# Table lookups with their row slots written out, and a reordered first row

## The chip, the cores and the metric

The kernel runs on one core of a Trainium2 chip, in one launch. The metric is the device time of that launch in microseconds (us); lower is better. The kernel before took 2431.6 us (median of 3 runs, 2429.14 to 2432.04).

The engines go by their short names: PE (matmuls), DVE (vector), ACT (scalar), POOL (GpSimd, which here issues the gathers) and SP (which issues the weight loads).

## The reference

Two transformer parts follow each other over 256 tokens of width 1024, all in f32: an FFN, latent and block attention and an FFN, then two layers of a mixer (a state-space mixer, then retention), a product-key lookup and a gated embedding. Only the two lookups matter here:

```python
def peer_ffn(h, w_q, sub_keys, u, v):            # T=256 tokens, 8 heads, K=16, NK=128
    q = (xt @ w_q).reshape(T, PEER_HEADS, 2, PEER_HALF)
    sc = jnp.einsum('thcd,hckd->thck', q, sub_keys)
    s1, i1 = lax.top_k(sc[:, :, 0], K)
    s2, i2 = lax.top_k(sc[:, :, 1], K)
    cand = (s1[..., :, None] + s2[..., None, :]).reshape(T, PEER_HEADS, K * K)
    cand_idx = (i1[..., :, None] * NK + i2[..., None, :]).reshape(T, PEER_HEADS, K * K)
    top_s, top_pos = lax.top_k(cand, K)
    idx = jnp.take_along_axis(cand_idx, top_pos, axis=-1)
    gate = jax.nn.softmax(top_s, axis=-1)
    ...
        hid = jax.nn.gelu(jnp.einsum('tkd,td->tk', u[ib], xb), approximate=False)
        return jnp.einsum('tk,tkd->td', (gb * hid), v[ib])
```

Each token and head picks 16 of 16384 rows of `u` and `v`, takes the dot product of the `u` row with the token, and adds up the `v` rows.

## The kernel before, in words

A stage `peer(layer)` does one lookup. The 256 tokens are 2 tiles of 128 partitions; a **row** is one tile and one head, so there are 16 rows, and a row has 16 **slots**, one for each chosen table row: 256 slots in a layer. Buffers for 8 gathered slots stand in SBUF (`SLOTS`), the matrices of the last four slots too (`DIAGS`).

A slot passes through all engines in this order. POOL waits until the buffer is free (`slot_free`) and issues an indirect DMA (L640), 128 descriptors of 8 KB, a `u` row and a `v` row each. DVE waits for it to land (`row_landed`) and takes the dot product (L1837). ACT applies gelu to the 128 sums (L1092). DVE writes a diagonal matrix of gelu times weight (`spread`, L1786). PE multiplies it with the `v` halves into two accumulating banks (L1907) and frees the buffer.

Between these, DVE chooses the experts of the **next** row (`pick`, a generator of 15 steps, one or two of which run in each slot), and ACT takes its softmax (`softmax_exp`, L1042) after slot 7; DVE makes the weights (`weigh`) in slot 10. Beside the slots (`beside`) PE multiplies the queries and scores of heads 2 to 7, for which SP loads a weight unit of 1 MB each, ACT writes its high part (L694) and DVE its low part (`split`, L1186). `HEAD_AT` gives the slot at which each head's product begins: 1, 13, 25, 40, 56, 72.

Row 0 has its own start. DVE copies its scores from a bank (L1676) and finds the first 8 experts (`first_pick`), so that POOL can issue 8 gathers, and the other 8 after them. `row_gain` (L1258) multiplies the token rows by the norm's gain, which the dot products need.

How the slots are written: `peer_rows` (L666) writes pairs of rows 0 to 4 out one after the other (`PAIRS_APART = 5`), and pairs 5 to 7 as one hardware loop of three turns (`Fori`, L670) on PE, DVE and ACT. In the loop the semaphore values to wait for are computed in registers. POOL writes its first pair out and loops seven times over the others (L646). Each engine runs its own program in its own order; nothing but semaphores ties them.

Of the kernel before, what the change touches and what calls it, by code (L numbers as in the profile page):

```python
# [90 lines left out]
SLOTS = 8  # L91
# [3 lines left out]
EARLY_HEADS = 2  # L95
# [7 lines left out]
PAIRS_APART = 5  # L103
# [106 lines left out]
def build(nc, x, pos_row, pos_col, consts_d, ret_consts_d, vecs_d, gains_d, gain_cols_d, wide_d, units_d, conv_d, pt_d, uv0, uv1, out):  # L210
    with ExitStack() as ctx:
# [409 lines left out]
        def _(pool):  # L621
            def gathers(layer):
# [3 lines left out]
                def two_rows(pair, i):  # L626
                    for par in range(2):
                        if pair == 0 and par == 0:
                            pool.wait_ge(expert_early, layer + 1)
                        else:  # L630
                            pool.wait_ge(expert_ready, i * 2 + (layer * (ROWS + 1) + 2 * pair + par + 1))
                        for k in range(TOPK):
# [4 lines left out]
                            pool.wait_ge(slot_free, i * (2 * TOPK) + (done + SLOTS * layer + (2 * pair + par) * TOPK + k + 1))  # L637
# [46 lines left out]
        def _(act):  # L684
# [337 lines left out]
            def peer(layer):  # L1022
# [65 lines left out]
                def two_rows(row, i, slot):  # L1088
                    for par in range(2):
                        for k in range(TOPK):  # L1090
                            act.wait_ge(dot_done, i * (2 * TOPK) + ((layer * ROWS + row + par) * TOPK + k + 1))
                            nc.scalar.activation(act_h[par][:, k:k + 1], hid[par][:, k:k + 1], ACT.Gelu).then_inc(gelu_done, 1)  # L1092
                            if slot is not None:
                                beside(slot + par * TOPK + k)
                            if k == 7:
                                softmax_exp(i * 2 + (row + par + 1))

                peer_rows(act, two_rows)
# [71 lines left out]
        def _(dve):  # L1170
# [460 lines left out]
            def peer(layer):  # L1631
# [79 lines left out]
                def pick(row, par):  # L1711
# [9 lines left out]
                    step(V.tensor_copy(st[:, 0], score[:, bass.ds(row, 1), :].rearrange("p a (c k) -> p (a c) k", c=2)))  # L1721
# [100 lines left out]
                def two_rows(first, i, slots):  # L1822
                    tile = first // PEER_HEADS
                    for par in range(2):
                        row = first + par

                        ahead = pick(i * 2 + (row + 1), 1 - par)
                        n = None
                        if tile == 0:

                            dve.wait_ge(score_act, i * 2 + (9 * layer + row + 2))
                        for k in range(TOPK):
                            slot = k % SLOTS
                            dve.wait_ge(row_landed[slot], i * 64 + 16 * (layer * ROWS * 2 + 2 * row + k // SLOTS + 1))
                            if n is not None:
                                picked(i * 2 + (row + 1), n)
                            V.scalar_tensor_tensor(rows_uv[:, slot, 0:D], rows_uv[:, slot, 0:D], 1.0, xn[:, tile, :], ALU.mult, ALU.mult,  # L1837
                                                   accum_out=hid[par][:, k:k + 1]).then_inc(dot_done, 1)
                            n = next(ahead, None)
                            if k >= 1:  # L1840
                                if n is not None:
                                    picked(i * 2 + (row + 1), n)
                                spread(i * (2 * TOPK) + (row * TOPK + k - 1), par, k - 1)
                                n = next(ahead, None)
# [747 lines left out]
```

## Time and profile before

| | us |
|---|---|
| median of 3 runs | 2431.6 (2429.14 to 2432.04) |
| the profiled execution, its own time | 2434.31 |
| span of that execution, first to last instruction | 2432.5 |
| PE busy | 2112.4 |
| DVE busy | 1729.6 |
| DVE idle before L1837 for a gather | 207.5 in 226 waits |
| ACT busy | 787.0 |
| bytes moved by DMA | 726.75 MB |
| of these by the gathers' queue | 539.00 MB |

The profile is one execution. Times in a row count from the start of the span. A row of the time order has start, length, engine, line, operation, output <- input, and in square brackets how long the engine stood idle before it and what ended that. A row of a stretch has its bounds and length, the busy time of PE, of PE's weight loads (PEld), DVE, ACT and POOL, each with the number of instructions, then the granted clock of PE as a share of full speed, the busy share of the 16 DMA engines and GB/s. A DMA queue's row has packets, MB and its share of the 16 engines' time. In rows, "issue" is idle time that no semaphore or transfer explains. The first lookup stage runs from about 775 to 1466 us, the second from about 1723 to 2392 us.

### The profile page before, as it was taken

The numbers are of one execution on the slowest core, as the hardware profiler recorded it, in microseconds if no ns is written. First come the engines' busy times: TensorE is split into PE (matmuls) and PEld (weight loads), VectorE is DVE, ScalarE is ACT, GpSimd is POOL, SyncE is SP. The second block draws the span as 40 slices with busy tenths as digits, with TensorE's granted clock in tenths as the row PEclk, the third lists the DMA queues.
The fourth block names the chain that finished last, engine by engine and source line by source line (L and its number), as shares of the span: only waits on it lengthen the run. The fifth ranks groups of instructions, "written<-read, shape, count | busy, mean of one in ns | idle before, by whom it ended". The sixth has DMA issues, their size and how long they took to land.

```text
span 2432.5 us, 27876 instructions
## 1 busy us (share of the span) xinstructions
PE 2112.4 (87%) x9134; PEld 1378.4 (57%) x9134; DVE 1729.6 (71%) x3722; ACT 787.0 (32%) x1463; POOL 592.2 (24%) x520
## 2 busy tenths in 40 slices
PE   7999899999999888887886688999888897777877
PEld 7998789989877444432332236977544442222324
DVE  5555665558766878878886686646778888877786
ACT  4334653346564221212111116334412211111114
POOL 0000000000101444444443340000343444443440
PEclk9999999999999999999998899999999999999999
DMA  6554325544325999999998995534799999999995
GB/s 247 189 186 170 129 98 181 190 173 165 139 87 209 420 420 417 403 420 408 408 412 342 379 400 228 188 141 156 300 420 420 401 409 420 405 420 415 408 421 210
DMA packets 101205, 726.75 MB, mean 299 GB/s; under 512 B 11616, under 2 KB 11744, under 8 KB 13280
## 3 DMA queue, kind: packets, MB, share of 16 engines
q0 software_dynamic: 74016, 539.00, 54.2%
q1 hardware_dynamic: 25200, 181.41, 20.5%
q10 hardware_dynamic: 1872, 4.88, 0.6%
q8 instruction: 60, 0.98, 0.2%
q14 instruction: 57, 0.47, 0.1%
HBM read 724.21 MB, written 1.05 MB: 298 GB/s over the span
## 4 chain that ended last, share of the span: by engine, by line
PE 23%; DMA 20%; DVE 14%; issue 14%; ACT 2%; POOL 1%; DVEq 0%; POOLq 0%; ACTq 0%; SPq 0%
PE bank L1907 22%; DMA arena<-in_uv,expert 19%; DVE arena L1786 3%; DVE arena L1837 2%; POOL arena L640 1%; DVE arena L1759 1%; DVE arena L1763 1%; DVE sel_i L1765 1%; DVE top_i L1737 1%; DVE arena L1729 1%; DVE top_i L1727 1%; DVE top_v L1732 0%; DVE lw_rounded L1186 0%; DVE arena L1742 0%; DVE top_v L1724 0%
## 5 line engine op out<-in xcount | busy, mean ns | idle before, releaser
L1907 PE MATMUL bank<-arena 128*128 128x512 f32 (+4 forms) x2416 | 1075.1, 579 | 261.4 <-DVE arena L1786 254.9
L1907 PEld LDWEIGHTS bank<-arena 128*128 128x128 f32 (+2 forms) x2416 | 421.1, 194 | 825.7 <-DVE arena L1786 519.9
L640 POOL DMA_INDIRECT arena<-in_uv,expert x512 | 581.5, 1136 | 1175.2 <-PE bank L1907 667.6
L1837 DVE SCALAR_TENSOR_TENSOR arena<-arena,xn 128x1024 f32<-128x1024 f32 x512 | 626.6, 1224 | 243.3 <-DMA arena<-in_uv,expert 207.5
L1186 DVE TENSOR_TENSOR lw_rounded<-lw,w_hi 128x2048 fp32r<-128x2048 f32 x169 | 389.4, 2306 | 222.0 <-ACT w_hi L694 218.8
L1092 ACT ACTIVATE act_h<-hid 128x1 f32<-128x1 f32 x512 | 103.6, 203 | 1055.5 <-DVE arena L1837 1055.1
L1907 PE MATMUL bank<-xT_hi,w_hi 128*128 128x256 f32 x1320 | 414.3, 314 | 4.2 <-DVE xT_lo L1227 4.2
L694 ACT ACTIVATE w_hi<-lw 128x2048 fp32r<-128x2048 f32 x169 | 323.4, 1915 | 260.7 <-PE bank L1907 235.5
L1907 PE MATMUL bank<-xT_hi,lw_rounded 128*128 128x256 f32 x1320 | 374.5, 284 | 0.0
L1907 PE MATMUL bank<-xT_lo,w_hi 128*128 128x256 f32 x1320 | 374.5, 284 | 0.0
L1907 PEld LDWEIGHTS bank<-xT_hi,w_hi 128*128 128x128 f32 x1320 | 253.6, 192 | 28.9 <-issue 25.9
L1907 PEld LDWEIGHTS bank<-xT_lo,w_hi 128*128 128x128 f32 x1320 | 253.4, 192 | 23.8 <-issue 23.0
L1907 PEld LDWEIGHTS bank<-xT_hi,lw_rounded 128*128 128x128 f32 x1320 | 253.3, 192 | 0.1
L1907 PE MATMUL bank<-w_hi,arena_rounded 128*128 128x512 f32 (+1 forms) x680 | 228.8, 407 | 2.4 <-DVE arena_rounded L1203 2.4
L1786 DVE TENSOR_SCALAR arena<-consts,act_h,weight 128x128 f32<-128x128 f32 x512 | 180.9, 353 | 26.8 <-ACT act_h L1092 6.4
L656 POOL TENSOR_TENSOR arena<-arena,vecs 128x2048 f32<-128x2048 f32 x2 | 9.3, 4644 | 602.2 <-ACT arena L694 602.2
L1907 PE MATMUL bank<-w_hi,xT_hi 128*128 128x512 f32 (+2 forms) x368 | 144.6, 393 | 11.7 <-DVE xT_lo L1249 6.5
L1907 PEld LDWEIGHTS bank<-w_hi,arena_rounded 128*128 128x128 f32 x680 | 129.4, 191 | 34.8 <-issue 3.8
L1907 PE MATMUL bank<-w_hi,xT_lo 128*128 128x512 f32 (+2 forms) x368 | 139.0, 378 | 0.0
L1907 PE MATMUL bank<-lw_rounded,xT_hi 128*128 128x512 f32 (+2 forms) x368 | 138.9, 377 | 0.0
L1907 PE MATMUL bank<-lw_rounded,arena_rounded 128*128 128x512 f32 (+1 forms) x340 | 134.9, 397 | 0.0
L1907 PEld LDWEIGHTS bank<-w_hi,xT_hi 128*128 128x128 f32 x368 | 70.1, 190 | 27.9 <-DVE xT_lo L1249 7.6
(249 smaller groups left out, 1486.4 us busy)
## 6 DMA issues: line engine op xcount, KB each, us to landing
lw<-in_units SPq DMA_DIRECT2D x169, 1024.0 KB, 4.8
arena<-in_uv,expert POOLq DMA_INDIRECT x512, 12.2
wide<-in_wide POOLq DMA_DIRECT2D x2, 1024.0 KB, 10.5
gain<-in_gains ACTq DMA_DIRECT2D x4, 512.0 KB, 6.7
wide<-in_units SPq DMA_DIRECT2D x2, 1024.0 KB, 7.6
h<-in_x SPq DMA_DIRECT2D x2, 512.0 KB, 6.1
arena<-in_ret_consts ACTq DMA_DIRECT2D x1, 1024.0 KB, 4.7
out<-xn SPq DMA_DIRECT2D x2, 512.0 KB, 2.6
```

Source lines behind the costliest of these rows:

```text
L640: nc.gpsimd.indirect_dma_start(out=rows_uv[:, slot, :], out_offset=None, in_=table, in_offset=bass.IndirectOffsetOnAxis(ap=expert[par][:, ...
L694: return nc.scalar.activation(o, i, ACT.Copy)
L1092: nc.scalar.activation(act_h[par][:, k:k + 1], hid[par][:, k:k + 1], ACT.Gelu).then_inc(gelu_done, 1)
L1186: V.tensor_tensor(w_lo[:, u % RING, :], lw[:, u % RING, :], w_hi[:, no % HIGHS, :].bitcast(F32), ALU.subtract).then_inc(lo_ready, 1)
L1727: step(V.max_index(top_i[:, c, 0:8], top_v[:, c, 0:8], st[:, 0, c]))
L1729: step(V.match_replace(st[:, 1, c], top_v[:, c, 0:8], st[:, 0, c], LOWEST))
L1737: step(V.max_index(top_i[:, c, 8:], top_v[:, c, 8:], st[:, 1, c]))
L1759: step(V.tensor_tensor(hot[:, c], sel_f[:, c].unsqueeze(2).to_broadcast([P, TOPK, TOPK]), marks.unsqueeze(1).to_broadcast([P, TOPK, TOPK]) ...
L1763: step(V.tensor_tensor(hot[:, c], hot[:, c], top_f[:, c].unsqueeze(1).to_broadcast([P, TOPK, TOPK]), ALU.mult))
L1786: V.tensor_scalar(diag[:, k % DIAGS, :], ident, act_h[par][:, k:k + 1], weight[par][:, k:k + 1], ALU.mult, ALU.mult).then_inc(diag_ready, 1)
L1837: V.scalar_tensor_tensor(rows_uv[:, slot, 0:D], rows_uv[:, slot, 0:D], 1.0, xn[:, tile, :], ALU.mult, ALU.mult, accum_out=hid[par][:, k:k ...
L1907: return nc.tensor.matmul(o, lhsT, rhs, start=start, stop=stop, **more)
```

## The change

All 16 rows of both layers are written out on PE, DVE, ACT and POOL; the loops L646 and L670 and the register arithmetic of their waits are gone. Besides, at the start of each lookup stage: `row_gain` of the first tile stands ahead of `first_pick`; the low part of the weight unit of head 2 (the third head) moves on DVE from ahead of the first slot into slot 1; the choice for row 1 begins in slot 2 of row 0, and with it the wait for the scores of head 1 (`score_act`); on ACT the first softmax comes ahead of the high part of that unit, and the copy of head 1's scores goes behind the first gelu.

```diff
-PAIRS_APART = 5
+
+SECOND_FROM = 2
...
-                two_rows(0, 0)
-                with pool.Fori(0, ROWS // 2 - 1) as i:
-                    two_rows(1, i)
+                for pair in range(ROWS // 2):
+                    two_rows(pair)
...
-        def peer_rows(eng, rows):
-
-            for pair in range(PAIRS_APART):
-                rows(2 * pair, 0, 2 * TOPK * pair)
-            with eng.Fori(0, ROWS // 2 - PAIRS_APART) as i:
-                rows(2 * PAIRS_APART, i, None)
+        def peer_rows(rows):
+
+            for pair in range(ROWS // 2):
+                rows(2 * pair, 2 * TOPK * pair)
...
+                softmax_exp(0)
                 split(first + 4)
-                softmax_exp(0)
-                for i in range(1, EARLY_HEADS):
-                    queries(i)
-                    scores(i)
+                queries(1)
...
                 def beside(slot):
 
+                    if slot == 0:
+                        scores(1)
...
+                row_gain((N_PEER0, N_PEER1)[layer], 0)
                 first_pick()
-                row_gain((N_PEER0, N_PEER1)[layer], 0)
                 weigh(0, 0)
-                split(first_unit + 4)
...
-                        if slot == at - 3:
+                        if slot == max(at - 3, 1):
                             split(first_unit + 1 + head + 1)
...
-                        ahead = pick(i * 2 + (row + 1), 1 - par)
-                        n = None
-                        if tile == 0:
-
-                            dve.wait_ge(score_act, i * 2 + (9 * layer + row + 2))
+                        ahead = pick(row + 1, 1 - par)
+                        n, start = None, SECOND_FROM if row == 0 else 0
                         for k in range(TOPK):
                             slot = k % SLOTS
-                            dve.wait_ge(row_landed[slot], i * 64 + 16 * (layer * ROWS * 2 + 2 * row + k // SLOTS + 1))
+                            if tile == 0 and k == start:
+                                dve.wait_ge(score_act, 9 * layer + row + 2)
+                            dve.wait_ge(row_landed[slot], 16 * (layer * ROWS * 2 + 2 * row + k // SLOTS + 1))
...
-                            n = next(ahead, None)
+                            n = next(ahead, None) if k >= start else None
```

In the order of instructions below, a row is line, operation, output <- input, size, and the semaphores that it waits for. Line numbers of the changed kernel are lower by 3 or 5 around here (L1837 is L1832, L1786 is L1783).

**DVE at the start of the first layer's choice.** L1792 prepares constants, L1676 reads the first scores. Before:

```order
L1634 MEMSET arena 128x256
L1791 COPY consts<-consts 128x8 [waits dve_order]
L1792 TENSOR_SCALAR consts<-consts 128x8
L1676 COPY arena<-bank6 128x256 [waits first_scores,dve_order]
L1679 MAX top_v<-arena 128x8 [waits first_read]
```

Now:

```order
L1788 COPY consts<-consts 128x8 [waits dve_order]
L1789 TENSOR_SCALAR consts<-consts 128x8
L1255 TENSOR_TENSOR xn<-xn,gain 128x1024 [waits gain_loaded1,dve_order]
L1673 COPY arena<-bank6 128x256 [waits first_scores,dve_order]
L1676 MAX top_v<-arena 128x8 [waits first_read]
```

The gain (L1258, now L1255) stands ahead of the copy of the scores.

**DVE from the end of the first choice (L1673, now L1670) into the first slots.** Before:

```order
L1673 SCALAR_TENSOR_TENSOR expert0<-sel_i 128x8 [waits dve_order]
L1258 TENSOR_TENSOR xn<-xn,gain 128x1024 [waits gain_loaded1]
L1774 RECIPROCAL exp_inv<-exp_sum 128x1 [waits exp_ready,dve_order]
L1776 TENSOR_SCALAR weight0<-exps,exp_inv 128x16 [waits top_order]
L1186 TENSOR_TENSOR lw_rounded<-lw,w_hi 128x2048 [waits hi_ready]
L1837 SCALAR_TENSOR_TENSOR arena,hid0<-arena,xn 128x1024 [waits row_landed0,score_act]
L1721 COPY arena<-arena 128x256
L1837 SCALAR_TENSOR_TENSOR arena,hid0<-arena,xn 128x1024 [waits top_order,row_landed1]
L1724 MAX top_v<-arena 128x8 x2
L1786 TENSOR_SCALAR arena<-consts,act_h0,weight0 128x128 [waits slot_free,gelu_done,top_order]
L1727 MAX_INDEX top_i<-top_v,arena 128x8 x2
L1729 MATCH_REPLACE arena<-top_v,arena 128x128 x2
```

Now:

```order
L1670 SCALAR_TENSOR_TENSOR expert0<-sel_i 128x8 [waits dve_order]
L1771 RECIPROCAL exp_inv<-exp_sum 128x1 [waits exp_ready]
L1773 TENSOR_SCALAR weight0<-exps,exp_inv 128x16 [waits top_order]
L1832 SCALAR_TENSOR_TENSOR arena,hid0<-arena,xn 128x1024 [waits row_landed0]
L1832 SCALAR_TENSOR_TENSOR arena,hid0<-arena,xn 128x1024 [waits row_landed1]
L1783 TENSOR_SCALAR arena<-consts,act_h0,weight0 128x128 [waits slot_free,gelu_done]
L1183 TENSOR_TENSOR lw_rounded<-lw,w_hi 128x2048 [waits hi_ready]
L1832 SCALAR_TENSOR_TENSOR arena,hid0<-arena,xn 128x1024 [waits row_landed2,score_act]
L1718 COPY arena<-arena 128x256
L1783 TENSOR_SCALAR arena<-consts,act_h0,weight0 128x128 [waits slot_free,gelu_done,top_order]
L1721 MAX top_v<-arena 128x8 x2
L1832 SCALAR_TENSOR_TENSOR arena,hid0<-arena,xn 128x1024 [waits top_order,row_landed3]
```

Gain and low part (L1186, now L1183) are gone from ahead of the first dot product; the low part stands behind the first `spread`, and the choice for row 1 begins with the copy behind the third dot product.

**DVE at the place where the first layer's loop begins.** Before, with the loop's head (L670) and register instructions (`REGISTER_ALU`, `ISA`):

```order
L1837 SCALAR_TENSOR_TENSOR arena,hid1<-arena,xn 128x1024 [waits row_landed7]
L1786 TENSOR_SCALAR arena<-consts,act_h1,weight1 128x128 [waits slot_free,gelu_done] x2
L670 UNCONDITIONAL_BRANCH
L670 ISA
L1837 SCALAR_TENSOR_TENSOR arena,hid0<-arena,xn 128x1024 [waits row_landed0]
L1721 ISA
L1721 COPY arena<-arena 128x256
L1780 ISA [waits row_landed1]
L1837 SCALAR_TENSOR_TENSOR arena,hid0<-arena,xn 128x1024 [waits top_order]
L1724 MAX top_v<-arena 128x8 x2
L1780 REGISTER_ALU
L1784 ISA [waits top_order]
```

Now:

```order
L1832 SCALAR_TENSOR_TENSOR arena,hid1<-arena,xn 128x1024 [waits row_landed7]
L1783 TENSOR_SCALAR arena<-consts,act_h1,weight1 128x128 [waits slot_free,gelu_done] x2
L1832 SCALAR_TENSOR_TENSOR arena,hid0<-arena,xn 128x1024 [waits row_landed0]
L1718 COPY arena<-arena 128x256
L1832 SCALAR_TENSOR_TENSOR arena,hid0<-arena,xn 128x1024 [waits top_order,row_landed1]
L1721 MAX top_v<-arena 128x8 x2
L1783 TENSOR_SCALAR arena<-consts,act_h0,weight0 128x128 [waits slot_free,gelu_done,top_order]
L1724 MAX_INDEX top_i<-top_v,arena 128x8 x2
```

The branch and the register instructions are gone; the waits stand on the working instructions.

## Rows read from the trace of the kernel before

**Rows 1.** The page: span, engine share, DMA share in 40 slices.

```profile
span 2432.5 us, 27876 instructions
PE 2112.4 (87%) x9134; PEld 1378.4 (57%) x9134; DVE 1729.6 (71%) x3722; ACT 787.0 (32%) x1463; POOL 592.2 (24%) x520
...
DMA  6554325544325999999998995534799999999995
```

**Rows 2.** Both lookup stages: length, PE, PEld, DVE, ACT, POOL busy, clock, DMA, GB/s.

```profile
777.00:1466.00 689.00, 556.78 (x1472) 245.59 (x1472) 542.84 (x1447) 129.37 (x362) 293.16 (x256) 0.95 0.99 402
1725.00:2392.00 667.00, 541.00 (x1465) 240.13 (x1465) 540.97 (x1442) 128.99 (x361) 286.48 (x255) 0.98 1.01 413
```

**Rows 3.** Waits of DVE: who, for whom, total us, times, longest.

```profile
DVE arena L1837 <- issue: 22.0, 2, 11.0
```

**Rows 4.** DVE in time order, first layer: around both jumps back, and the loop's end.

```profile
1287.45 0.35 DVE L1786 TENSOR_SCALAR arena<-consts,act_h,weight 128x128 f32<-128x128 f32 x1 [0.45 <-ACT act_h L1092]
1298.79 1.22 DVE L1837 SCALAR_TENSOR_TENSOR arena<-arena,xn 128x1024 f32<-128x1024 f32 x1 [11.00 <-issue]
...
1376.10 0.35 DVE L1786 TENSOR_SCALAR arena<-consts,act_h,weight 128x128 f32<-128x128 f32 x1 [0.45 <-ACT act_h L1092]
1387.46 1.22 DVE L1837 SCALAR_TENSOR_TENSOR arena<-arena,xn 128x1024 f32<-128x1024 f32 x1 [11.01 <-issue]
...
1465.02 0.35 DVE L1786 TENSOR_SCALAR arena<-consts,act_h,weight 128x128 f32<-128x128 f32 x1 [0.45 <-ACT act_h L1092]
```

**Rows 5.** The same in the second layer.

```profile
2233.75 0.79 DVE L1786 TENSOR_SCALAR arena<-consts,act_h,weight 128x128 f32<-128x128 f32 x2
2235.10 1.23 DVE L1837 SCALAR_TENSOR_TENSOR arena<-arena,xn 128x1024 f32<-128x1024 f32 x1 [0.56 <-DMA arena<-in_uv,expert]
...
2313.88 0.79 DVE L1786 TENSOR_SCALAR arena<-consts,act_h,weight 128x128 f32<-128x128 f32 x2
```

**Rows 6.** DMA from 1287 to 1312 us: share in 40 slices; instruction queue.

```profile
DMA  9999999999999999999997210000000000077799
...
q14 instruction: 4, 0.03, 0.3%
```

**Rows 7.** DMA queues from 820 to 1206 us, rows written out.

```profile
q14 instruction: 11, 0.09, 0.1%
```

**Rows 8.** Stretches in the loops, and one of written-out rows (last).

```profile
1206.30:1286.30 80.00, 65.62 (x127) 23.53 (x125) 63.46 (x171) 12.23 (x39) 35.44 (x32) 0.91 1.01 414
...
2153.00:2233.00 80.00, 60.33 (x127) 21.88 (x126) 62.91 (x171) 12.22 (x39) 33.07 (x32) 1.00 1.01 416
2233.00:2313.00 80.00, 62.37 (x129) 22.91 (x128) 63.96 (x175) 12.43 (x40) 35.42 (x32) 0.98 1.01 411
...
2115.00:2153.00 38.00, 28.77 (x61) 9.96 (x60) 32.17 (x92) 7.54 (x25) 15.55 (x16) 1.00 1.01 421
```

**Rows 9.** DVE before the first slots of both layers, in time order.

```profile
768.98 0.17 DVE L1792 TENSOR_SCALAR consts<-consts 128x8 f32<-128x8 f32 x1
770.45 0.42 DVE L1676 COPY arena<-bank 128x256 f32<-128x256 f32 x1 [1.30 <-PE bank L1907]
...
785.72 1.22 DVE L1258 TENSOR_TENSOR xn<-xn,gain 128x1024 f32<-128x1024 f32 x1
...
787.31 2.29 DVE L1186 TENSOR_TENSOR lw_rounded<-lw,w_hi 128x2048 fp32r<-128x2048 f32 x1
790.10 1.22 DVE L1837 SCALAR_TENSOR_TENSOR arena<-arena,xn 128x1024 f32<-128x1024 f32 x1 [0.50 <-ACT arena L694]
...
1718.32 0.42 DVE L1676 COPY arena<-bank 128x256 f32<-128x256 f32 x1 [1.58 <-PE bank L1907]
```

**Rows 10.** DMA queues from 777 to 806 us.

```profile
q0 software_dynamic: 1151, 8.43, 72.9%
q1 hardware_dynamic: 432, 3.15, 26.2%
```

**Rows 11.** DVE at the ninth slot of the first row.

```profile
812.93 1.23 DVE L1837 SCALAR_TENSOR_TENSOR arena<-arena,xn 128x1024 f32<-128x1024 f32 x1 [0.71 <-DMA arena<-in_uv,expert]
```

More of the change, by code:

```diff
@@ L630, in two_rows @@
                         else:
-                            pool.wait_ge(expert_ready, i * 2 + (layer * (ROWS + 1) + 2 * pair + par + 1))
+                            pool.wait_ge(expert_ready, layer * (ROWS + 1) + 2 * pair + par + 1)
                         for k in range(TOPK):
@@ L1086, in beside, with two_rows @@
                         high_tile((N_PLE0, N_PLE1)[layer], 0, (slot - HIGH_AT,))
-                def two_rows(row, i, slot):
+                def two_rows(row, slot):
                     for par in range(2):
                         for k in range(TOPK):
-                            act.wait_ge(dot_done, i * (2 * TOPK) + ((layer * ROWS + row + par) * TOPK + k + 1))
+                            act.wait_ge(dot_done, (layer * ROWS + row + par) * TOPK + k + 1)
                             nc.scalar.activation(act_h[par][:, k:k + 1], hid[par][:, k:k + 1], ACT.Gelu).then_inc(gelu_done, 1)
-                            if slot is not None:
-                                beside(slot + par * TOPK + k)
+                            beside(slot + par * TOPK + k)
                             if k == 7:
-                                softmax_exp(i * 2 + (row + par + 1))
-                peer_rows(act, two_rows)
+                                softmax_exp(row + par + 1)
+                peer_rows(two_rows)
             def ple(layer):
@@ L1719, in pick @@
                     flat = [cand[:, i].rearrange("p a b -> p (a b)") for i in range(2)]
-                    step(V.tensor_copy(st[:, 0], score[:, bass.ds(row, 1), :].rearrange("p a (c k) -> p (a c) k", c=2)))
+                    step(V.tensor_copy(st[:, 0], score[:, row, :].rearrange("p (c k) -> p c k", c=2)))
                     yield 1
@@ L1820, in add_tile, with two_rows @@
                     add_to_h([(2 * tile + c, tile, c * BANK) for c in range(2)])
-                def two_rows(first, i, slots):
+                def two_rows(first, slots):
                     tile = first // PEER_HEADS
@@ L1840, in two_rows @@
                             if k >= 1:
                                 if n is not None:
-                                    picked(i * 2 + (row + 1), n)
-                                spread(i * (2 * TOPK) + (row * TOPK + k - 1), par, k - 1)
-                                n = next(ahead, None)
+                                    picked(row + 1, n)
+                                spread(row * TOPK + k - 1, par, k - 1)
+                                n = next(ahead, None) if k >= start else None
@@ L1845, in two_rows @@
                             if k == 10:
-                                weigh(i * 2 + (row + 1), 1 - par)
-                            if slots is not None:
-                                beside(slots + par * TOPK + k)
-                        spread(i * (2 * TOPK) + (row * TOPK + TOPK - 1), par, TOPK - 1)
-                peer_rows(dve, two_rows)
+                                weigh(row + 1, 1 - par)
+                            beside(slots + par * TOPK + k)
+                        spread(row * TOPK + TOPK - 1, par, TOPK - 1)
@@ L2465, in beside, with two_rows @@
                         turn_tile((N_PLE0, N_PLE1)[layer], 0)
-                def two_rows(row, i, slots):
+                def two_rows(row, slots):
                     tile = row // PEER_HEADS
@@ L2470, in two_rows @@
                         for k in range(TOPK):
-                            pe.wait_ge(diag_ready, i * (2 * TOPK) + ((layer * ROWS + row + par) * TOPK + k + 1))
+                            pe.wait_ge(diag_ready, (layer * ROWS + row + par) * TOPK + k + 1)
                             for c in range(2):
@@ L2475, in two_rows @@
                             ins.then_inc(slot_free, 1)
-                            if slots is not None:
-                                beside(slots + par * TOPK + k)
-                peer_rows(pe, two_rows)
+                            beside(slots + par * TOPK + k)
+                peer_rows(two_rows)
             def ple(n):
```

7 lines of the change are left out of this document (4 added, 3 removed).

## The prediction

> **What bounds the kernel now.** I read the page first, for where the DMA engines are full. The span is 2432.5 us, PE is busy for 87% of it, and that invites a wrong reading: in slices 13 to 23 and 29 to 38 (counted from 0), the two lookups, the DMA digit is 9 or 8, and PE and DVE only keep up with the gathers [rows 1]. The second view was the busy time by stretch. The first lookup stage, 777 to 1466 us, moves 402 GB/s, the second, 1725 to 2392 us, does the same work in 667 us at 413 GB/s [rows 2]. Undisturbed written-out rows reach 421 GB/s [rows 8]. So a lookup stage costs its bytes over some 420 GB/s, plus the time in which the DMA engines run dry. An edit here is worth what it takes from the dry time, and nothing else: a shorter DVE or ACT path that ends before the next gather lands only makes DVE wait longer for it.
>
> The third view was DVE's waits, to find who lets the DMA engines run dry. One line stands out: two waits for nothing that the profile shows, 11.0 us each [rows 3]. In order of time they lie in the first layer only, between the last diagonal of a row and the first dot product of the next, where DVE's loop L670 jumps back [rows 4]. In that time no diagonal is made, PE frees no buffer and POOL has nothing to issue; the transfers under way go on until 1300 us and then stop: the DMA digits are 2, 1 and then ten zeros of 0.6 us each, and in the same stretch four packets go over the instruction queue [rows 6]. That is an instruction fetch: the code to which DVE jumps has to be brought in again. In the second layer the same jump leaves DVE waiting 0.56 us, for a gather [rows 5]. In written-out rows, 820 to 1206 us, 11 packets of instructions come and none makes DVE wait [rows 7, 3].
>
> **The price of the loops, step by step.** An iteration of the loop is two rows. From the end of the last diagonal before a jump to the same point one iteration on, the first layer takes 1376.45 - 1287.80 = 88.65 us and 1465.37 - 1376.45 = 88.92 us [rows 4], start plus length. The second layer takes 2314.67 - 2234.54 = 80.13 us for the same work without the pause [rows 5]. The pauses of 11 us each cost 8.5 and 8.8 us at the end; the rest is covered by transfers already issued. Sum 17.3 us. The whole stages say the same: 689 us at 402 GB/s are 277.0 MB, at the other stage's 413 GB/s 670.7 us, 18.3 us less, in which other differences between the layers are included [rows 2]. I take 17.3. This is the whole of the main term, and it is in one layer only. What is late next there is what is late in the second layer: the gather's landing, 0.56 us.
>
> The second term is the register arithmetic of the loop's waits. In the second layer's loop the rate is 416 and 411 GB/s over 80 us each, in the first layer's first iteration 414, against 421 in written-out rows [rows 8]. Against 420 that is (4/420 + 9/420 + 6/420) x 80 = 3.6 us for three of the six iterations, so 7 us at most if the register instructions were the cause of all of it, and nothing if it is the dense half of each row (choice steps beside dot products), which the written-out rows have as well. Written-out rows differ in this too, so I take 1.7 us, nearer to nothing. That the code is longer afterwards (six more rows on three engines, fourteen on POOL) costs fetches of the kind in rows 7: 8 KB each in a stream of 420 GB/s, 0.02 us.
>
> By the Trainium skill, "Runtime: NRT & Kernel Launch", section "Instruction fetch mechanics", straight code is streamed ahead and its block crossings are mostly hidden, while a taken branch to a block outside the current window must fetch first. The trace agrees for written-out rows and for the first layer's jumps, and does not for the second layer's, which cost nothing; had both layers' jumps stalled as the rule may be read, the gain would be 35 us. The section also gives 16 KiB blocks; here four packets of 8 KB come at one jump [rows 6].
>
> **The reordered start.** Four edits, in each layer, one answer. The gain's product takes 1.22 us [rows 9]. Ahead of the first choice it falls into a time in which DVE waits for the first scores: 1.30 us before 770.45 and 1.58 us before 1718.32 [rows 9]. It fits in both, in the first layer by 0.08 us, so the first gather is issued where it was, or up to 0.1 us later. Behind the choice DVE then drops 1.22 us for the gain, 2.29 us for the low part of head 2 and the 0.50 us wait for the scores of head 1 [rows 9]: the first dot product moves from 790.10 to about 786.4 us. Slot 1 takes the low part, so the third dot product comes at least 3.7 - 2.3 = 1.4 us earlier than before, somewhat more since the choice's first steps now stand behind it, and with it the freeing of the first buffers. The exponentials needed for the first weight must be ready then; ACT now makes them before the high part instead of after it, and even in the old order they did not hold DVE, whose only idle time there is the 0.50 us. The moved wait for head 1's scores stands ahead of the third dot product, and all later slots queue behind it on DVE; the scores were there at 790.10, some 2 us before it is reached.
>
> What does the end see of that? The ninth gather is issued some 2 us earlier, but the DMA engines are not dry there: from 777 to 806 us they move 8.43 MB of gathers and 3.15 MB of weight units [rows 10], which is 11.6 MB or 27.6 of 29 us at 420 GB/s. By the ninth slot DVE waits for the landing, 0.71 us [rows 11], and the head start has become a longer wait. The choice for row 1 now ends after the tenth dot product instead of the eighth. POOL needs it with the buffer of the ninth slot, whose diagonal DVE writes just behind that point, so it is not late. I take 0 for all four. Bounds: +0.2 us for both layers if the gain delays the first choice; -7.4 us if the whole 3.7 us moved through to the end twice.
>
> **The sum.** 17.3 + 1.7 + 0 = 19.0 us. The profiled execution took 2434.31 us, 1.8 us more than its span, which the change leaves alone: 2415.3. The median of the runs shown is 2.7 us lower, so for timed runs 2431.6 - 19.0 = 2412.6 us.
>
> **Rivals.**
> The head start arrives (A). Mechanism: with buffers freed earlier, the queue of gathers is deeper through the dense rows 1 to 5, where the DMA engines also run dry now and then; the second stage has 667 us where 275.5 MB at 420 would take 656, and the first keeps about as much once its pauses are gone [rows 2]. For it: these 11 us a layer are there to be had. Against: DVE waits for gathers in the second half of each row, which forgets the head start. Time: 2412.6 - 7 = 2405.6.
>
> The pauses go but part comes back (B). The first layer's rows 12 to 15 would have dry spells of their own, as the second layer has with no pause (411 GB/s over 80 us), hidden now because all buffers are full after a pause. For it: the second layer shows them. Against: the comparison of iterations already includes them. If 5 of the 19 us return: 2417.6.
>
> The change does nothing to the pauses (C). If the fetch were not caused by the jump but by something at this place in the stream, the written-out code would meet it too: 2431.6 less 1.7, about 2430. Against: both pauses stand at a jump, none in 20 written-out rows.
>
> Slower (D). Written-out code misses its fetch where the loop of the second layer ran from what was there. New are 6 rows on DVE, PE and ACT in each layer, about one fetch per row on DVE by the 11 packets in nine rows [rows 7]. Twelve fetches that each held DVE 11 us as a jump does, at 8.7 us each at the end, are 104 us for 17.3 saved. It decides from the third such miss on (26 > 19); at four, 2431.6 + 34.8 - 19 = 2447.4. For it: the queue is full of gathers when the fetch is asked for. Against: 20 written-out rows of the same code under the same load show none, which leaves little room.
>
> **How the numbers follow.** Forecast with all its terms 0.76, A 0.09, B 0.09, C 0.03, D 0.03. No change within 0.2% (4.9 us, about what a measurement of this kernel can tell from none) is C. Faster takes forecast, A and B: 0.94; same 0.03; slower 0.03. Range: low end all of A, 2405; high end B and a spread of 1.5 us between runs, 2419.
>
> **What would show it.** In the profile after: no wait of DVE for "issue" of 11 us; the first lookup stage about 671 us long at 412 GB/s or more; no zeros in the DMA digits between the stage's ends; the second stage 664 to 667 us. The first gather within 0.1 us of where it was relative to the first scores, the first dot product within 1 us of the choice's last instruction (now 4.4 us, 785.72 to 790.10), and a DVE wait for a landing by the ninth slot longer than 0.71 us. I am wrong if the first stage stays above 680 us, if the second gets shorter than 660 or longer than 670 us, or if DVE waits for "issue" in written-out rows.

## The result, and the profile after

The changed kernel takes 2419.4 us (median of 5 runs, 2418.2 to 2420.9), the kernel before 2431.6 (2429.1 to 2434.6, 5 runs beside them); the ratio is 0.995, 95% interval 0.9935 to 0.9965. It is faster by 12.2 us, where 19.0 were forecast (2412.6, range 2405 to 2419). The direction and the main term were right; a cost that the forecast put at almost nothing took back about a third of it and moved the time just outside the range.

The page of the profile after, which answers to [rows 1]: span, engines, DMA share in 40 slices, and the instruction queues.

```profile
span 2417.6 us, 26693 instructions
PE 2100.5 (87%) x9134; PEld 1369.8 (57%) x9134; DVE 1730.7 (72%) x3722; ACT 786.6 (33%) x1463; POOL 584.6 (24%) x520
...
DMA  6554325544325999999999994533899999999994
...
q8 instruction: 64, 1.05, 0.2%
q14 instruction: 58, 0.48, 0.1%
```

Both lookup stages by stretch, which answers to [rows 2] (columns as there):

```profile
774.00:1448.00 674.00, 543.31 (x1473) 239.80 (x1474) 543.21 (x1450) 129.52 (x364) 285.58 (x257) 0.99 1.00 412
1707.00:2379.00 672.00, 546.70 (x1470) 240.62 (x1470) 543.01 (x1449) 129.45 (x365) 288.07 (x256) 0.98 1.00 411
```

From the first packet of a stage's gathers to its last dot product, the first stage went from 685.8 to 670.1 us and the second from 667.5 to 669.3: at 412 and 411 GB/s they are now alike, and the second has become slower. DVE's waits, largest first, no longer have the line of [rows 3]:

```profile
DVE arena L1832 <- DMA arena<-in_uv,expert: 219.9, 233, 3.2
DVE lw_rounded L1183 <- ACT w_hi L692: 217.6, 100, 6.1
DVE arena L1287 <- ACT arena L775: 40.5, 21, 2.0
```

At the place of the first jump [rows 4] DVE now goes from diagonal to dot product with a wait of 0.64 us, for a gather:

```profile
1282.76 0.70 DVE L1783 TENSOR_SCALAR arena<-consts,act_h,weight 128x128 f32<-128x128 f32 x2
1284.10 1.23 DVE L1832 SCALAR_TENSOR_TENSOR arena<-arena,xn 128x1024 f32<-128x1024 f32 x1 [0.64 <-DMA arena<-in_uv,expert]
```

So the pauses went. What is missing shows when row is set beside row, by the start of each row's first dot product. Rows 13 to 15 of the second layer, in the loop before, took 39.9 us each, 16 gathers at 2.49 us; written out they take 40.9. The 2.49 us are what the packets give: 128 descriptors of 8 KB over 16 DMA engines are 8 packets each, at 0.31 us per packet in the trace (that each engine gets 8 is an estimate).

### The profile page after: what moved, and what is told of

Same layout as the page of the kernel before. It is cut to its first block, busy times and chain, and to the rows that moved or that the text cites. A ratio compares the mean times of both kernels' runs of the same rounds, so it can differ in the third digit from the quotient of the medians.

```text
span 2417.6 us, 26693 instructions
## 1 busy us (share of the span) xinstructions
PE 2100.5 (87%) x9134; PEld 1369.8 (57%) x9134; DVE 1730.7 (72%) x3722; ACT 786.6 (33%) x1463; POOL 584.6 (24%) x520
## 4 chain that ended last, share of the span: by engine, by line
PE 23%; DMA 22%; DVE 14%; issue 12%; ACT 2%; POOL 1%; DVEq 0%; POOLq 0%; ACTq 0%; SPq 0%
PE bank L1901 22%; DMA arena<-in_uv,expert 22%; DVE arena L1783 3%; DVE arena L1832 2%; POOL arena L641 1%; DVE top_i L1734 1%; DVE arena L1756 1%; DVE arena L1726 1%; DVE top_i L1724 1%; DVE arena L1760 1%; DVE sel_i L1762 1%; DVE top_v L1729 0%; DVE top_v L1721 0%; DVE lw_rounded L1183 0%; DVE sel_s L1737 0%
## 5 line engine op out<-in xcount | busy, mean ns | idle before, releaser
L1901 PE MATMUL bank<-arena 128*128 128x512 f32 (+4 forms) x2416 | 1062.9, 572 | 257.0 <-DVE arena L1783 250.6
L1901 PEld LDWEIGHTS bank<-arena 128*128 128x128 f32 (+2 forms) x2416 | 413.1, 192 | 817.7 <-DVE arena L1783 522.8
L641 POOL DMA_INDIRECT arena<-in_uv,expert x512 | 573.8, 1121 | 1168.4 <-PE bank L1901 641.7
L1832 DVE SCALAR_TENSOR_TENSOR arena<-arena,xn 128x1024 f32<-128x1024 f32 x512 | 626.9, 1225 | 238.7 <-DMA arena<-in_uv,expert 219.9
L1183 DVE TENSOR_TENSOR lw_rounded<-lw,w_hi 128x2048 fp32r<-128x2048 f32 x169 | 389.4, 2306 | 220.7 <-ACT w_hi L692 217.6
L1783 DVE TENSOR_SCALAR arena<-consts,act_h,weight 128x128 f32<-128x128 f32 x512 | 181.6, 355 | 18.3 <-ACT act_h L1090 9.8
```

What stands on the lines that cost most here:

```text
L641: nc.gpsimd.indirect_dma_start(out=rows_uv[:, slot, :], out_offset=None, in_=table, in_offset=bass.IndirectOffsetOnAxis(ap=expert[par][:, ...
L1183: V.tensor_tensor(w_lo[:, u % RING, :], lw[:, u % RING, :], w_hi[:, no % HIGHS, :].bitcast(F32), ALU.subtract).then_inc(lo_ready, 1)
L1783: V.tensor_scalar(diag[:, k % DIAGS, :], ident, act_h[par][:, k:k + 1], weight[par][:, k:k + 1], ALU.mult, ALU.mult).then_inc(diag_ready, 1)
L1901: return nc.tensor.matmul(o, lhsT, rhs, start=start, stop=stop, **more)
```

## The experiments

All times are medians of 4 to 11 runs, but for two single runs near the end, beside runs of the kernel before on the same chip, whose medians there were 2430.3 to 2432.1 us. "Piece" below is 128 instructions of DVE's code, the 8 KB that one packet of the instruction queue brings.

**The loop's place alone.**

```diff
-            with eng.Fori(0, ROWS // 2 - PAIRS_APART) as i:
+            heads = {eng.engine: 0} if eng.engine == mybir.EngineType.DVE else None
+            with nc.Fori(0, ROWS // 2 - PAIRS_APART, engines=..., head_slot=heads) as i:
```

> The kernel before with one thing changed: the first instruction of DVE's loop in each lookup stage is placed at slot 0 of a block of 256 instructions; nothing is written out and the start is the old one. In the kernel before the loop of layer 0 begins with the last instruction before a boundary of 128 (DVE executes one instruction after the jump and then stands still), so that its 260 instructions touch four pieces of 128, and the loop of layer 1 (267 instructions) touches three. Theory (place of the loop, and written-out code is not free): both 11-us pauses go without any code written out, and rows 10 to 15 keep the 39.9 us per row of layer 1's loop, so 2431.6 - 17.3 = 2414.3 us, range 2412.5 to 2416, some 5 us under the written-out kernel although nothing of its other gains is in. Rival 1 (the jump itself stalls in layer 0 wherever it lies): 2431.6, pauses still there. Rival 2 (pauses go, but they were worth only the 12.2 us that writing out brought): 2419 to 2420.

Measured: 2419.5 us. The 11-us pauses are gone with nothing written out, so the jump itself does not stall. But placing the loop this way makes DVE jump into it, which costs a new wait in each layer. DVE's time order, the first dot product of the loop in both layers:

```profile
1209.42 1.22 DVE L1838 SCALAR_TENSOR_TENSOR arena<-arena,xn 128x1024 f32<-128x1024 f32 x1 [5.30 <-issue]
2141.45 1.22 DVE L1838 SCALAR_TENSOR_TENSOR arena<-arena,xn 128x1024 f32<-128x1024 f32 x1 [5.29 <-issue]
```

The time is what rival 2 gave, but its reason is not: rows 13 to 15 are at 39.9 us here, and the same placing without the jump (the padded loop, below) is 5.5 us faster. That the time equals the changed kernel's is a coincidence of two costs.

**The pauses carried to the other layer.** As above, but `head_slot` 13 and layer 0 alone.

> The kernel before, with DVE's loop of layer 0 alone placed, at slot 13 of a block of 256 instructions. Layer 0's 260 instructions then touch three pieces of 128; layer 1's loop, which stands 109 slots further on modulo 128, comes to slot 122 and its 267 instructions touch four. Theory (the number of pieces of 128 that the body touches decides): the two 11-us pauses vanish from layer 0 and appear in layer 1: stage 0 shrinks from 689 to 671 us, stage 1 grows from 667 to some 684, total 2431.6 - 17.3 + 17.3 = 2431.6, range 2429 to 2434. Rival 1 (something of layer 0 causes the pauses): 2431.6 with the pauses still in layer 0. Rival 2 (any placed loop is free, the neighbour does not matter): 2414.3 with no pause at all.

Measured: 2431.0 us, ratio 1.000 (0.9991 to 1.0009), the pauses in layer 1. DVE there, around both jumps back:

```profile
2213.75 0.79 DVE L1787 TENSOR_SCALAR arena<-consts,act_h,weight 128x128 f32<-128x128 f32 x2
2220.75 1.22 DVE L1838 SCALAR_TENSOR_TENSOR arena<-arena,xn 128x1024 f32<-128x1024 f32 x1 [6.21 <-issue]
2225.61 1.22 DVE L1838 SCALAR_TENSOR_TENSOR arena<-arena,xn 128x1024 f32<-128x1024 f32 x1 [3.42 <-issue]
...
2301.31 0.79 DVE L1787 TENSOR_SCALAR arena<-consts,act_h,weight 128x128 f32<-128x128 f32 x2
2308.27 1.22 DVE L1838 SCALAR_TENSOR_TENSOR arena<-arena,xn 128x1024 f32<-128x1024 f32 x1 [6.17 <-issue]
2313.13 1.23 DVE L1838 SCALAR_TENSOR_TENSOR arena<-arena,xn 128x1024 f32<-128x1024 f32 x1 [3.43 <-issue]
```

The place of the loop in memory is the cause: it now spans a fourth piece in layer 1 and not in layer 0. The pause is in two parts, 6.2 us in which two packets of instructions come (2216.2 and 2218.7 us) and 3.4 us in which one does (2223.7); the fourth, at 2228.8, holds nothing up. I read them as the wait for the piece with the head and the wait for the next, with the few instructions between them that stand before the boundary. In the kernel before there was one such instruction, and the two waits read as one of 11.0 [rows 4]. The two halves of this exchange are not equal in the trace: layer 0's stage is 17.6 us shorter than in the kernel before, layer 1's 12.8 us longer. A placed loop as such is not free of it (rival 2 falls).

**The loop placed by padding.** DVE runs through the padding, so nothing jumps into the loop.

```diff
+            if eng.engine == mybir.EngineType.DVE and layer == 0:
+                eng.addr_align(128)
             with eng.Fori(0, ROWS // 2 - PAIRS_APART) as i:
```

> The kernel before, with DVE's loop of layer 0 moved to the next multiple of 128 instructions by padding that DVE runs through (about one instruction), so that the loop is entered without a jump; layer 1's loop moves along by the same amount and still touches three pieces. Nothing written out, old start. Theory: no 11-us pause, and none of the 5.3-us waits that entering the jumped-to loops cost in the first experiment. There rows 9 and 10 took 44.6 + 37.5 us in layer 0 and 45.5 + 39.2 in layer 1, against 39.9 + 40.9 and 40.9 + 40.9 without such a wait: 1.3 + 2.9 us to be had. 2419.5 - 4.2 = 2415.3 us, range 2413.5 to 2417.5, faster than the changed kernel. Rival (a wait of 5.3 us is covered by the full queue of gathers and comes back in the next row): 2419.5.

Measured: 2414.1 us (2412.3 to 2415.6), ratio 0.9928 (0.9915 to 0.9942), 17.4 us less than before with two empty instructions more. That is the price that the forecast put on the pauses, 17.3, measured alone.

**The jump announced.** The loops where they were, with `hint_back_edge` on DVE's, one instruction at the head of the loop that names the target of the jump back.

> The kernel before, its loops where they were, with one more instruction at the head of DVE's loop that announces the jump back (a prefetch of its target). If the pause is the wait for a fetch that starts only with the jump, it goes; the four packets per jump are still fetched, so the stream may pay for them: 2414 + 0 to 8 = 2414 to 2422 us. If the announcement does nothing, or DVE cannot hold what it fetches ahead: about 2431, pauses of 11 us. The two extra instructions also shift the code: layer 0's head stays at its place, layer 1's moves by one, which by the count of pieces changes nothing.

Measured: 2413.3 us (2411.9 to 2415.2), ratio 0.9928 (0.9913 to 0.9943), the fastest of all with the one above. DVE's waits, and the DMA queues from the loop's first jump back to the end of layer 0's stage (1284 to 1444 us):

```profile
DVE lw_rounded L1187 <- ACT w_hi L695: 214.8, 98, 5.0
DVE arena L1838 <- DMA arena<-in_uv,expert: 201.0, 223, 2.2
DVE arena L1291 <- ACT arena L778: 40.7, 21, 2.1
```

```profile
q0 software_dynamic: 9035, 65.74, 99.2%
q1 hardware_dynamic: 157, 1.18, 1.9%
```

No pause at the jumps, and no packet of instructions at all, where I had expected four per jump. How the announcement keeps the head from being fetched again is not settled by this.

**Which engine's written-out code costs.** On top of the padded loops, all rows written out on PE, ACT and POOL, or on DVE alone.

```diff
+            written = {PE, Activation, DVE} - {DVE}        # the other kernel: {DVE}
+            if eng.engine in written:
+                for pair in range(PAIRS_APART, ROWS // 2):
+                    rows(2 * pair, 0, 2 * TOPK * pair)
+                return
```

> As the kernel with the padded loop, but PE, ACT and POOL have all rows written out and DVE alone keeps its loops. If the 1.0 us by which written-out rows 13 to 15 are longer (40.9 against 39.9 us) comes from DVE's fetches, the rows stay at 39.9 and the time is that of the padded loops, about 2415.3; if it comes from the fetches of PE, ACT or POOL, they take 40.9 and the time is 4 to 6 us more, 2420.

> The other half: DVE alone has all rows written out, PE, ACT and POOL keep their loops; old start. If DVE's fetches (one piece of 128 instructions per row) make the difference: rows 13 to 15 at 40.9 us and the time of the changed kernel, 2419 to 2420.5. If the others' fetches do: rows at 39.9 and some 2415.

Measured: 2415.3 and 2421.2 us, against 2414.1 with the padded loops. It is DVE's code: 7.2 us for six rows in each layer, while the 1.2 us of the others lie within the scatter of the runs. The stretch of rows 13 to 15 of layer 0 in the changed kernel, then in the padded one:

```profile
1325.00:1447.80 122.80, 92.56 (x193) 33.22 (x192) 96.27 (x261) 18.63 (x60) 43.77 (x44) 1.00 0.99 404
```

```profile
1326.10:1445.80 119.70, 93.18 (x193) 33.90 (x192) 95.89 (x261) 18.64 (x60) 45.43 (x44) 0.99 1.01 418
```

Same instructions and busy times, 3.1 us apart. The DMA queues of the same stretches: in the changed kernel

```profile
q8 instruction: 2, 0.03, 0.1%
q14 instruction: 4, 0.03, 0.1%
```

and none of the two in the padded one. Packet by packet: DVE's fetch of 1342.90 us in the changed kernel takes 0.33 us, and a packet of a gather that starts as it ends takes 0.97 instead of 0.31. The records do not name the DMA engine of a packet; if the two share one, it loses 1.0 us. Three of the four packets on q14 here have a mark close to this one, and the rows are 3.1 us longer. From the third dot product after it DVE waits. The changed kernel, then the padded one, at the same two slots of row 13:

```profile
1346.37 1.22 DVE L1832 SCALAR_TENSOR_TENSOR arena<-arena,xn 128x1024 f32<-128x1024 f32 x1
1348.42 1.23 DVE L1832 SCALAR_TENSOR_TENSOR arena<-arena,xn 128x1024 f32<-128x1024 f32 x1 [0.56 <-DMA arena<-in_uv,expert]
1350.92 1.28 DVE L1832 SCALAR_TENSOR_TENSOR arena<-arena,xn 128x1024 f32<-128x1024 f32 x1 [1.00 <-DMA arena<-in_uv,expert]
```

```profile
1347.78 1.22 DVE L1839 SCALAR_TENSOR_TENSOR arena<-arena,xn 128x1024 f32<-128x1024 f32 x1
1349.18 1.22 DVE L1839 SCALAR_TENSOR_TENSOR arena<-arena,xn 128x1024 f32<-128x1024 f32 x1
1351.04 1.23 DVE L1839 SCALAR_TENSOR_TENSOR arena<-arena,xn 128x1024 f32<-128x1024 f32 x1 [0.37 <-DMA arena<-in_uv,expert]
```

The two spacings are 2.05 + 2.50 us against 1.40 + 1.86.

**More of DVE's fetches.** The changed kernel, with DVE's slots 8 to 15 of rows 8 to 15 padded.

```diff
+                            if row >= 8 and k >= 8:
+                                dve.addr_align(16)
```

> The changed kernel, with empty instructions on DVE: in slots 8 to 15 of rows 8 to 15 of both layers each slot is padded to 16 instructions, some 11 more, which DVE runs through in 0.6 us of the 1.0 us that it waits there for a gather. That is 88 instructions per row, 0.69 of a piece of 128, 5.5 more fetches by DVE in each layer. Theory (each fetch of DVE's code costs the gather stream 1.0 us: 0.33 us for itself and 0.66 us by which the next packet on its DMA engine is longer): 11 more fetches, 2419.4 + 11 = 2430 us, rows at 41.6 on average. Rival 1 (it is not the fetches but something else in written-out DVE code): 2419.4. Rival 2 (only the bytes count): 2419.6.

Measured: 2430.9 us, 11.5 more than the changed kernel. The instruction queues over rows 8 to 15 of layer 0, changed kernel and then this one:

```profile
q8 instruction: 4, 0.07, 0.1%
q14 instruction: 10, 0.08, 0.1%
```

```profile
q14 instruction: 15, 0.12, 0.1%
q8 instruction: 4, 0.07, 0.1%
```

Five more fetches, and the stage, counted as above, went from 670.1 to 675.7 us; in layer 1 five more again, 669.3 to 675.2. It is the fetches and not the time of the empty instructions: all eight rows have the padding, but they took 41.8, 41.1, 41.8, 41.2, 41.9, 40.9 and 42.0 us from row 9 on, long where a second piece of DVE's fell into the row. A fetch costs some 1.0 us by the rows and 1.1 to 1.2 by the stages.

**Other engines' fetches.** SP running through waits already met, PE and ACT through padding.

```diff
+                    for _ in range(256):                # SP, after a gather of rows 8 to 15
+                        sp.wait_ge(x_loaded[0], 16)
...
+                            if row >= 8:
+                                pe.addr_align(16)       # the other kernel: act
```

> The changed kernel with extra instructions on SP and nothing else: while it waits for the end of a lookup stage, it runs through 128 instructions that wait for nothing, once per row in rows 8 to 15 of layer 0 and twice per row in layer 1, so that some 8 and 16 more pieces of 8 KB are fetched, none of them for an engine that works. Theory A (each fetch holds up the gather stream by 0.97 us, whoever asks): rows 8 to 15 take 41.9 us in layer 0 and 42.9 in layer 1 instead of 40.9; 2419.4 + 8 x 0.97 + 16 x 0.97 = 2442.7 us. Theory B (a fetch takes its time from one of the 16 DMA engines, another for SP than for DVE, and the engine with most fetches sets the pace): rows stay 40.9 in layer 0, 41.9 in layer 1, 2427 us. Theory C (only the bytes count, as predicted): 24 x 8 KB at 412 GB/s = 0.5 us, 2419.9. Theory D (only DVE's own fetches cost, through DVE): 2419.4.

> The changed kernel, with the same on PE: in rows 8 to 15 each slot is padded to 16 instructions, some 11 more, 176 per row, 0.69 of a piece of 256 (16 KB). PE waits 1.0 us per slot there, so its own time does not count. Each such fetch takes 1.06 us and makes the next packet 0.5 us longer, so with one per row PE's DMA engine would lose 1.55 us per row, more than DVE's 1.0. Theory B (the DMA engine that loses most sets the pace): rows at 41.4, 2419.4 + 16 x 0.55 = 2428 us. Theory D (only DVE's fetches are paid for, as SP's extra ones left the rows at 40.9): 2419.4.

Measured: 2437.6 and 2421.8 us. SP's kernel did not do quite what was meant: its extra instructions and their packets show only in rows 12 to 15 of each layer, so that there are two pieces per row in layer 0 and four in layer 1. Why none shows in rows 8 to 11 is open. The total misleads. The rows up to 14 hold; row 15 of layer 1 is 1.4 us longer than in the changed kernel. What grew by 17 us is the part behind the last lookup, because SP still runs through its last instructions before it may issue the final stage's loads (the first at 2392.6 us instead of 2375.1). From the last dot product to the end, changed kernel and then this one:

```profile
2377.60:2417.60 40.00, 30.23 (x127) 22.66 (x125) 23.41 (x32) 23.77 (x36) 0.00 (x0) 0.95 0.29 122
```

```profile
2378.70:2435.60 56.90, 32.92 (x127) 24.70 (x125) 23.59 (x32) 23.64 (x36) 0.00 (x0) 0.81 0.23 93
```

Rows 13 and 14 of layer 1 take 81.8 us in both, with 3 packets on the queue in the one and 11 in the other. PE's extra pieces (8 for 4 in rows 8 to 15) leave the rows at 40.9 too, although by their mark they lose 1.55 us per row, more than DVE's: the engine that loses most does not set the pace at once, as theory B has it. That left open whether only DVE's fetches are paid for, or whether these were too few. So two more kernels, SP again without the piece at the end:

> The changed kernel with extra instructions on SP in rows 8 to 14 of both layers: four pieces of 128 per row, none behind the last landing, so that the next stage's loads are not held up (with two per row the rows stayed at 40.9 us). In the records an SP fetch takes 0.31 us and the next packet 0.41 us more, 0.72 in all, so 2.9 us per row. If that hits one and the same DMA engine each time and an engine's loss in a row beyond DVE's 1.0 us is paid for: rows at 42.8, 14 rows x 1.9 = 27 us more, 2446. If SP's fetches are never paid for, at four per row either: rows at 40.9 and 2419 to 2421.

> The changed kernel with each of ACT's slots in rows 8 to 15 padded to 16 instructions, run through while ACT waits for the next dot product; some 1.5 more pieces of 128 per row. ACT's fetches show 0.31 us and 0.38 more on the next packet, 0.7 each. If any engine's fetch were paid for like DVE's: 24 more fetches, 17 us, 2436. If only DVE's are: rows at 40.9, 2419 to 2421.

Measured, one run each: 2544.1 and 2419.3 us. SP's instructions start late here too (its packets from row 12 on) and take longer than the rows do, so that they ran on some 60 us past each stage; the total says nothing, the rows do. Rows 13 and 14, in layer 0 and in layer 1:

```profile
1324.40:1410.40 86.00, 64.85 (x130) 22.97 (x129) 64.32 (x175) 12.43 (x40) 34.31 (x33) 0.96 1.00 404
```

```profile
2319.30:2405.10 85.80, 66.77 (x131) 24.01 (x130) 64.49 (x174) 12.42 (x40) 36.13 (x33) 0.94 1.00 402
```

4 us more than 81.8. SP now fetches a piece every 8.2 us, five per row at 0.72 us each: 3.6 us over the 39.9, and rows 14 and 15 took 43.5 to 44.2. From then on the dot product after each SP fetch comes 3.21 us after the one before it, 2.49 + 0.72. With ACT's two per row, 1.4 us, rows 13 to 15 of layer 0 take 41.3 (123.85 us together) and those of layer 1 stay at 40.9. This fits one reading: each engine's code comes over its own DMA engine, a gather has landed when the slowest of the 16 has done its share, and the others run some us ahead of DVE's, a lead that a few fetches use up first (as in row 15 of layer 1 above). Which packets share a DMA engine is not in the records, and the lead that PE's eight rows would need was not measured, so that reading is argued, not shown. That not only DVE's fetches are paid for is shown by SP's.

**The start.** Three pairs of kernels differ in the start alone.

> The changed kernel's start of each lookup stage, with the loops of the kernel before on all engines and DVE's loop heads placed at slot 0 of a block of 256 instructions. Theory: the start brings some 1.7 us per layer (read from the difference of the two traces at the first rows) and the placed loops bring 17.3 us without the 1 us per row that written-out rows 12 to 15 lose: 2431.6 - 17.3 - 3.4 = 2410.9 us, range 2409 to 2414, faster than the changed kernel's 2419.4 by 8 us. My prediction's own terms (start worth nothing): 2414.3. Rival (written-out code costs nothing, something else eats the gain): 2419.

> The changed kernel with all rows written out, but the old start of each stage (gain behind the first choice, low part of the third head ahead of the first slot, choice for row 1 and its wait from the first slot on, ACT's old order). As predicted (the start is worth nothing): 2419.4 us. By the traces' difference of 1.5 to 1.9 us per layer at the first rows: 2422.6, range 2421.5 to 2424. If the whole 3.7 us came through twice: 2426.8.

> The padded loops (2414.07 us) with the changed kernel's start of each stage. As predicted (the start is worth nothing): 2414.1. By the pair of written-out kernels (old start 2420.45, new start 2419.37): 1 us less, 2413.0. By the pair of placed loops (2419.54 and 2420.30): 0.8 us more, 2414.8. The three together say whether the sign is anything but scatter; range 2412 to 2416.

Measured, old start and new: placed loops 2419.5 and 2420.3; written out 2420.5 and 2419.4; padded 2414.1 and 2414.8 us. The differences are +0.8, -1.1 and +0.7, scatter around nothing. My reading of the two traces, 1.7 us a layer, fell.

## Why the prediction was right or wrong

**The pauses, 17.3 us: right,** and measured alone at 17.4. Their cause was right too (a fetch), but "the code to which DVE jumps has to be brought in again" was only half of it: the same jump is free where the loop's body touches three pieces and not four.

**"That the code is longer afterwards ... costs fetches ...: 8 KB each in a stream of 420 GB/s, 0.02 us": this step failed.** I priced a fetch by its bytes at the rate of all 16 DMA engines together. One packet of 8 KB takes 0.31 to 0.33 us in the trace, and the one behind it is longer too: DVE's fetches cost 1.0 us each of the gather stream. Writing its six rows out cost 7.2 us in the timed runs, 5 of them in the two stages of the traces (2.0 and 3.0). The trace before had it: in layer 1 the looped rows 13 to 15 took 39.9 us, the written-out rows 3 to 9 between 40.9 and 41.2, but for row 7, the one without a fetch of DVE's, with 39.8; for the first layer [rows 7] counts the fetches. I took 421 GB/s for written-out rows from one stretch of 38 us [rows 8], too short to tell (the row in which it lies took 40.9 us like the others), and read the loop's 411 as the loop's fault. Had I compared whole rows, the term would have been six rows by 1.0 in each layer less the three pieces of the loop's first pass: about 3 x 2 = 6 us, and the forecast 17.3 - 6 = 11.3 us saved, 12.2 measured. That sum is made after the fact.

**Register arithmetic, 1.7 us: nothing.** In the dense slots of a looped row the dot products stand 2.60, 3.18, 3.01, 2.96 us apart, written out 2.50, 3.16, 3.00, 2.94 (row 13 of layer 0), but the row's second half waits for gathers and gives it back: a looped row without a fetch takes 39.9 us, a written-out one 39.8 or 39.9.

**The start, 0: right at the end, though not as argued.** The first gather comes 5.1 us after the copy of the scores, before and after, and the gain fits as worked out: in layer 1 the wait is now 0.31 us.

```profile
1701.55 0.42 DVE L1673 COPY arena<-bank 128x256 f32<-128x256 f32 x1 [0.31 <-PE bank L1901]
```

The first dot product starts 0.14 us after DVE's last instruction of the first weight, 10.5 us after the first gather instead of 14.5 [rows 9]. But then DVE waits 2.83 us for ACT, which still has the high part (1.90 us), a wait of 1.85 us for PE, a copy and a table load ahead of the first gelu:

```profile
787.16 0.60 ACT L692 ACTIVATE arena<-bank 128x512 f32<-128x512 f32 x1 [1.85 <-PE bank L1901]
787.78 1.28 ACT L1090 ACT_TABLE_LOAD   x1
789.07 0.20 ACT L1090 ACTIVATE act_h<-hid 128x1 f32<-128x1 f32 x1
...
789.31 0.35 DVE L1783 TENSOR_SCALAR arena<-consts,act_h,weight 128x128 f32<-128x128 f32 x1 [2.83 <-ACT act_h L1090]
...
811.87 1.22 DVE L1832 SCALAR_TENSOR_TENSOR arena<-arena,xn 128x1024 f32<-128x1024 f32 x1
```

That gelu starts 15.5 us after the first gather, before 15.8, so that of the 4 us 0.3 are left. The tenth dot product, that of [rows 11] (the prediction took it for the ninth slot's), is 0.9 us later after the first gather than before (38.25 against 37.34) and waits for nothing. So the head start was not lost in a longer wait for a landing, as I wrote, but in a wait for gelu and, as I read it, in the choice's steps that moved behind it. Rival A had nothing to pass on.

**The rest of the working.** Of the rivals, B came nearest in time (2417.6) by another mechanism: no dry spells, but fetches. D's fear, fetches that hold DVE itself, did not occur: no wait for "issue" in any written-out row. Its place was right and its victim wrong, the stream instead of the engine. Of my signs two failed: the longer wait by the ninth slot, and the second stage at 664 to 667 us (669.3 as counted above), which pointed to the cause.

## What to carry to other kernels

Where DMA engines are the bound, straight code is not free: count an engine's pieces of 128 instructions and price each by the spacing of whole repeated units (rows here) with and without one, not by its bytes. When a loop pauses at its jump, move or announce it before writing it out; here two empty instructions saved 5 us more than hundreds of written-out ones. And compare the same row of two stages before calling a stretch undisturbed.

## What the runs showed of the hardware

- A DVE loop of 260 to 267 instructions ran without a fetch when it touched three pieces of 128, and fetched four packets at each jump when it touched four: 11.0 us of pause in the kernel before, 6.2 + 3.4 us when its head lay six instructions ahead of the boundary. The Trainium skill, "Runtime: NRT & Kernel Launch", section "Instruction fetch mechanics", says that a taken branch outside the window of two pages of 256 instructions must fetch; here the step from three pieces to four decided, by packets of 128.
- A jump forward, into a loop placed at slot 0 or 13 of a block, cost DVE 5.3 us.
- The Trainium skill, in the same section, calls the cost of crossing a block in straight code mostly hidden and gives fetch stalls as a reason to unroll. Hidden from DVE it was, in every row; from the gather stream it was not, at 1.0 us per piece, and unrolling was the slower of the two cures.
- Most of an engine's fetches have the same mark, the time of the packet and of the gather's packet that starts as it ends: DVE's 0.33 and 0.97 us (some 0.31 and 0.84 to 0.94), SP's 0.31 and 0.72, ACT's 0.31 and 0.69, PE's 16 KB 1.06 and 0.8. A gather's packet usually takes 0.31.
